# A two-layer decoder trunk on one NeuronCore: the per-layer gates in two halves of 512 columns, and p loaded earlier

## The reference, cut to what matters

```python
x = layer_norm(DEEPNORM_ALPHA * x + mix, ln1_g[i], ln1_b[i])
hid = jnp.square(jax.nn.relu(jnp.einsum('bsd,df->bsf', x, ffn_w1[i])))
x = layer_norm(DEEPNORM_ALPHA * x + jnp.einsum('bsf,fd->bsd', hid, ffn_w2[i]), ln2_g[i], ln2_b[i])
gate = jax.nn.sigmoid(jnp.einsum('bsd,de->bse', x, ple_gate_w[i]))
x = x + gate * jnp.einsum('bsk,kd->bsd', p[i], ple_w[i])
```

## Time and profile before

| | |
|---|---|
| median of 3 runs | 2124.36 us (2123.57 to 2124.47) |
| profiled execution | 2122.74 us, its span 2121.0 us |
| TensorE busy | 2102.9 us, 99% of the span |
| VectorE, ScalarE, GpSimd busy | 1270.7, 792.8, 733.5 us |
| granted TensorE clock | 1.00 (2.4 GHz) |
| chain of waits that ended last | PE 91%, DVE 3%, DMA 2% |

### The profile page before, as it was taken

How to read it: one execution, slowest core, us unless ns; L and a number is a source line. 1 busy time by engine, 2 the same in 40 slices (tenths; PEclk the granted TensorE clock), 3 DMA queues, 4 the chain that set the end, 5 groups by cost and what they waited for, 6 DMA issues and landing times.

```text
span 2121.0 us, 27192 instructions
## 1 busy us (share of the span) xinstructions
PE 2102.9 (99%) x10565; PEld 1786.2 (84%) x10565; DVE 1270.7 (60%) x1747; ACT 792.8 (37%) x1197; POOL 733.5 (35%) x493
## 2 busy tenths in 40 slices
PE   9999999999999999999999999999999999999999
PEld 9887788888888888899888888788888888888899
DVE  5744776565667666565543352676556667666564
ACT  3112464544544334521211101454454543344521
POOL 5112157777512000212432222258777512000220
PEclk9999999999999999999999999999999999999999
DMA  5121124444599743301121111124444599643311
GB/s 184 39 62 46 35 80 149 141 148 163 180 361 380 248 155 129 129 26 46 41 80 40 57 43 48 32 80 161 155 141 148 203 381 378 228 131 130 129 38 73
DMA packets 185948, 287.31 MB, mean 135 GB/s; under 512 B 12800, under 2 KB 82524, under 8 KB 185820
## 3 DMA queue, kind: packets, MB, share of 16 engines
q1 hardware_dynamic: 185120, 285.26, 39.4%
q10 hardware_dynamic: 700, 0.31, 0.1%
HBM read 221.56 MB, written 63.96 MB: 135 GB/s over the span
## 4 chain that ended last, share of the span: by engine, by line
PE 91%; DVE 3%; DMA 2%; issue 1%; POOL 1%; ACT 1%; SPq 0%; DVEq 0%; POOLq 0%; ACTq 0%
PE bank_a L1785 16%; PE bank_a L1787 16%; PE bank_a L1786 16%; PE bank_b L1785 14%; PE bank_b L1787 14%; PE bank_b L1786 14%; PE bank_a L1824 1%; DMA w_raw<-in_ffn_w_dram 1%; DMA p_n<-in_p_dram 1%; PE bank_b L1824 1%; DVE xt_lo L1339 0%; DVE xt_hi L1334 0%; POOL op_lo L983 0%; PE bank_a L1994 0%; DMA h_spill<-h_tile 0%
## 5 line engine op out<-in xcount | busy, mean ns | idle before, releaser
L968 POOL TENSOR_TENSOR w_lo<-raw,w_hi 128x512 fp32r<-128x512 f32 x160 | 226.3, 1446 | 986.0 <-ACT w_hi L1072 985.9
L1785 PE MATMUL bank_a<-xt_hi,w_hi 128*128 128x512 f32 x640 | 251.4, 393 | 2.7 <-DVE xt_lo L1339 2.7
L1787 PE MATMUL bank_a<-xt_hi,w_lo 128*128 128x512 f32 x640 | 249.2, 389 | 0.0
L1786 PE MATMUL bank_a<-xt_lo,w_hi 128*128 128x512 f32 x640 | 249.1, 389 | 0.0
L1526 DVE TENSOR_TENSOR hop_lo<-h_raw,hop_hi 128x1024 fp32r<-128x1024 f32 x112 | 141.6, 1265 | 141.8 <-ACT hop_hi L1165 141.6
L1165 ACT CAST hop_hi<-h_raw 128x1024 fp32r<-128x1024 f32 x112 | 117.7, 1051 | 237.4 <-PE bank_a L1787 140.6
L1785 PE MATMUL bank_a<-wop_hi,hop_hi 128*128 128x512 f32 x512 | 199.3, 389 | 0.7 <-DVE resid L1551 0.7
L1786 PE MATMUL bank_a<-wop_lo,hop_hi 128*128 128x512 f32 x512 | 199.2, 389 | 0.0
L1787 PE MATMUL bank_a<-wop_hi,hop_lo 128*128 128x512 f32 x512 | 199.2, 389 | 0.0
L1072 ACT CAST w_hi<-raw 128x512 fp32r<-128x512 f32 x160 | 88.2, 620 | 266.1 <-PE bank_a L1787 154.7
L1785 PE MATMUL bank_b<-w_hi,xt_hi 128*128 128x256 f32 x640 | 182.4, 285 | 2.3 <-DVE xt_lo L1339 1.7
(11 more groups left out here) (190 smaller groups left out, 4961.9 us busy)
## 6 DMA issues: line engine op xcount, KB each, us to landing
w_raw<-in_ffn_w_dram SPq DMA_DIRECT2D x144, 512.0 KB, 7.6
h_raw<-h_spill SPq DMA_DIRECT2D x112, 512.0 KB, 6.5
h_spill<-h_tile SPq DMA_DIRECT2D x170, 256.0 KB, 2.2
w_raw<-in_ffn_w_dram SPq DMA_DIRECT2D x112, 256.0 KB, 3.5
raw<-in_od_w_in_dram SPq DMA_DIRECT2D x48, 256.0 KB, 2.8
raw<-in_ple_gate_w_dram SPq DMA_DIRECT2D x32, 256.0 KB, 4.8
h_spill<-h_tile2t SPq DMA_DIRECT2D x28, 256.0 KB, 2.0
raw<-in_ev_w_in_dram SPq DMA_DIRECT2D x24, 256.0 KB, 3.1
```

Of the source, the lines that this page charges most:

```text
L968: pool.tensor_tensor(w_lo[slab % 2][:, s], raw[:, n % NRAW, :], w_hi[slab % 2][:, s].bitcast(F32), ALU.subtract).then_inc(lo_split, 1)
L1785: pe.matmul(dst, s_hi, m_hi, start=first, stop=False, skip_group_check=on_top)
L1786: pe.matmul(dst, s_hi, m_lo, start=False, stop=False, skip_group_check=on_top)
L1787: return pe.matmul(dst, s_lo, m_hi, start=False, stop=last, skip_group_check=on_top)
```

## The change

The gates of a layer are computed in two halves of 512 columns. A half's weights are ten pieces (eight of the gate's, two of p's), each 128 rows by 512 columns. A tile's gate product takes a whole bank and its p product the next one. The first half's pieces lie in the two slabs; six of the second half's lie in new places between 152 and 176 KB and four in the second slab, which TensorE gives back piece by piece during the last tile of the first half (`gate_step`). The sigmoid's buffer is twice as wide. p's load moves from `second` to the front of `slab`, and the turning of its first half from inside the last item to behind item 53. Because p then lies in 168 to 176 KB from there on, the w2 pieces of the last form take turns in 128 and 132 alone. ScalarE splits the second slab once item 55 is prepared, where it waited for item 55's difference alone. In layer 1 the stores go by halves. The diff, cut to its core:

```diff
@@ -189,7 +189,7 @@
     def w_chunk(self, load):
         if load < self.first_load[LAST_FORM]:
             return (184, 188, 32, 36, 168, 172, 176, 180)[load % 8]
-        return (128, 168, 172, 132, 128, 132, 168, 172)[load - self.first_load[LAST_FORM]]
+        return (128, 132)[(load - self.first_load[LAST_FORM]) % 2]
 
     def w_landed(self, load):
         return load % 8, 16 * (self.layer * self.loads // 8 + load // 8 + 1)
...
@@ -273,7 +273,7 @@
         st.need_x, st.need_h, st.turned = list(need["xu"]), list(need["hu"]), list(turned)
         adds = dict(ADDS.get(kind, {}))
         if kind in ("out", "gate", "v"):
-            adds["gb"] = adds["bread"] = len(args["tiles"]) * (2 if kind == "out" else 1)
+            adds["gb"] = adds["bread"] = len(args["tiles"]) * (1 if kind == "v" else 2)
             if kind == "gate":
                 adds["xnew"] = len(args["tiles"])
             if args.get("sums") is not None:
...
@@ -434,9 +434,9 @@
             if i == LAST_FORM + 3:
                 add("slab", layer=layer, load_next=True, split_next=True)
             if i == LAST_FORM + 5:
+                add("turn_p", half=0, layer=layer)
                 add("second", layer=layer)
-        st.inner = [add("turn_p", half=0, layer=layer, nested=True, early=True)]
-        squares_of(hi).inner = st.inner
+        squares_of(hi)
         add("stats", half=1, ln=ln)
         add("norm", half=1, ln=ln)
 
@@ -453,16 +453,25 @@
         add("prep", item=n, layer=layer)
 
     def gates(layer):
-        for c in range(4):
-            slab = ("gate", layer, c)
-            if c == 0:
-                token_halves("gate", slab, "ln", ln=2 * layer + 1, p=True, layer=layer, col=c)
-                continue
-            add("gate", slab=slab, tiles=lo, col=c, layer=layer)
-            if c == 3 and layer == 0:
-                last_half("gate", "gate", layer=layer, col=c)
-            else:
-                add("gate", tiles=hi, col=c, layer=layer, last=True)
+        add("more", slab=("gate", layer, 0), split_next=False, load_next=False)
+        add("gate", slab=("gate", layer, 1), tiles=[0, 1], layer=layer, split_next=False, load_next=False)
+        add("gload", layer=layer)
+        inner = [turns("ln", 1, list(range(KT)), ln=2 * layer + 1, nested=True)]
+        inner.append(add("turn_p", half=1, layer=layer, nested=True))
+        add("gate", tiles=[2, 3], inner=inner, layer=layer)
+        add("gsplit", item=0, layer=layer)
+        add("gate", tiles=hi[:-1], layer=layer)
+        add("gsplit", item=1, layer=layer)
+        add("gate", tiles=hi[-1:], layer=layer)
+        for _ in range(3):
+            slab_end.append(("gb", at["gb"]))
+        for c in (2, 3):
+            add("more", slab=("gate", layer, c), split_next=False, load_next=False)
+        st = add("gate", tiles=lo, col=1, layer=layer, split_next=True, load_next=True)
+        if layer == 0:
+            last_half("gate", "gate", layer=layer, col=1)
+        else:
+            add("gate", tiles=hi, col=1, layer=layer, last=True)
 
 
...
@@ -557,6 +566,9 @@
         tmp = at("tmp", [P, NTMP, HALF], 176 * K1)
         gb_rows = at("gb_rows", [P, 2, D], 192 * K1)
         shared = at("shared", [P, 512], 200 * K1)
+        sig = at("sig", [P, 2, HALF], 200 * K1)
+        g_hi = [at(f"g_hi{k}", [P, PIECE], a * K1, F32R) for k, a in enumerate((152, 156, 160, 164, 168, 172))]
+        g_lo = [at(f"g_lo{k}", [P, PIECE], a * K1, F32R) for k, a in enumerate((154, 158, 162, 166, 170, 174))]
         ws_t = at("ws_t", [P, 4, P], 202 * K1)
         ident = at("ident", [P, P], 206 * K1)
         small = 206 * K1 + 512
...
@@ -710,6 +722,21 @@
 
             q, f = {"A11": (0, 0), "A12": (1, 0), "A21": (0, 1), "A22": (1, 1)}[op]
             return w1_raw[b % 2][:, 4 * q:4 * q + 4, f * P:(f + 1) * P]
+
+        def piece_place(slab, q):
+
+            kind = slabs[slab][0]
+            if kind[0] == "gate" and kind[2] >= 2:
+                q += 5 * (kind[2] - 2)
+                if q < len(g_hi):
+                    return g_hi[q][:, :], g_lo[q][:, :]
+                slab, q = slab // 2 * 2 + 1, q - len(g_hi)
+            s = slice(q * PIECE, (q + 1) * PIECE)
+            return w_hi[slab % 2][:, s], w_lo[slab % 2][:, s]
+
+        def gate_slab(layer, c):
+
+            return next(i for i, (kind, _) in enumerate(slabs) if kind == ("gate", layer, c))
 
         def by_four(ap):
             return ap[:, :].rearrange("p (q f) -> p q f", q=4)
...
@@ -752,8 +779,9 @@
                     return row_slab(ev_w_out[0], what[1])
                 if kind == "od_out":
                     return row_slab(od_w_out[0], what[1])
-                ple = ple_w[what[1]].rearrange("(k p) n -> p k n", p=P)
-                return column_slab(ple_gate_w[what[1]], what[2] * BLK) + [ple[:, :, bass.ds(what[2] * BLK, BLK)]]
+                half, ks = what[2] // 2, range(5 * (what[2] % 2), 5 * (what[2] % 2) + 5)
+                return [(ple_gate_w if k < KT else ple_w)[what[1]][bass.ds(k % KT * P, P), half * HALF:(half + 1) * HALF]
+                        for k in ks]
 
             def load_slab(what, piece):
                 for q, src in enumerate(sources(what)):
...
@@ -843,13 +871,15 @@
                 if st.kind == "slab":
 
                     sp.wait_ge(ahead_dve, ahead[st.layer].dve[LAST_FORM - 1])
+                    sp.dma_start(p_n[:, :, :], p[st.layer, 0].rearrange("(t q) k -> q t k", q=P)).then_inc(p_in, 16)
                 if st.load_next and st.cur + 1 < n_slabs:
                     load_slab(*slabs[st.cur + 1])
+                if st.kind == "gload":
+                    load_slab(slabs[st.cur + 1][0], st.piece)
+                    load_slab(slabs[st.cur + 2][0], st.piece + 5)
                 if st.kind == "second":
-
                     load_slab(slabs[st.cur + 2][0], st.piece + 5)
                     sp.wait_ge(ahead_dve, ahead[st.layer].dve[-1])
-                    sp.dma_start(p_n[:, :, :], p[st.layer, 0].rearrange("(t q) k -> q t k", q=P)).then_inc(p_in, 16)
                     load_gb(ln2_g[st.layer], ln2_b[st.layer], D)
                 if st.kind == "ffn":
                     for k in range(2):
...
@@ -997,6 +1026,11 @@
                     split_low(st.cur + 2, st.piece + 4, 4)
                 if st.kind == "second":
                     split_low(st.cur + 2, st.piece + 5, 5)
+                if st.kind == "gsplit" and st.item == 0:
+                    split_low(st.cur + 1, st.piece, 5)
+                    split_low(st.cur + 2, st.piece + 5, 1)
+                if st.kind == "gsplit" and st.item == 1:
+                    split_low(st.cur + 2, st.piece + 6, 4, at=1)
                 if st.kind == "wsum" and ITEMS[st.item][0] == "m6":
                     a, i = ahead[st.layer], st.item
                     for n in range(2):
...
@@ -1136,8 +1170,19 @@
                 fifth = st.split_next and st.cur + 1 < n_slabs and slabs[st.cur + 1][0][0] == "gate"
                 if st.kind == "split":
                     split_high(st.cur + 2, st.piece + 4, 4, slab_end[st.cur])
+                if st.kind == "gsplit" and st.item == 0:
+                    split_high(st.cur + 1, st.piece, 5)
+                    split_high(st.cur + 2, st.piece + 5, 1)
+                if st.kind == "gsplit" and st.item == 1:
+                    for q in range(4):
+
+                        if q == 2:
+                            act.wait_ge(b_full, st.gb + 1)
+                        else:
+                            act.wait_ge(gate_step, 3 * st.layer + min(q, 2) + 1)
+                        split_high(st.cur + 2, st.piece + 6 + q, 1, at=1 + q)
                 if st.kind == "second":
-                    act.wait_ge(ahead_dve, ahead[st.layer].sum[-1])
+                    act.wait_ge(ahead_dve, ahead[st.layer].dve[-1])
                     split_high(st.cur + 2, st.piece + 5, 4)
                     split_high(st.cur + 2, st.piece + 9, 1, at=4)
                 if st.kind == "consts":
...
@@ -1291,14 +1336,14 @@
                         if k == len(st.tiles) - 1:
                             for turn in st.inner if len(st.tiles) == HT else ():
                                 values(turn)
-                        act.wait_ge(b_full, st.gb + k + 1)
+                        act.wait_ge(b_full, st.gb + 2 * k + 1)
                         if st.xnew + k >= 2:
 
                             act.wait_ge(x_new, st.xnew + k - 1)
                         else:
 
                             act.wait_ge(a_full, st.ga)
-                        act.activation(sig[:, (st.xnew + k) % 2, :], bank_b[(st.gb + k) % RING][:, 0:BLK],
+                        act.activation(sig[:, (st.xnew + k) % 2, :], bank_b[(st.gb + 2 * k) % RING][:, :],
                                        ACT.Sigmoid).then_inc(sig_ready, 1)
                 if fifth:
                     split_high(st.cur + 1, st.piece + 4, 1, at=4)
...
@@ -1760,10 +1802,10 @@
```

(61 more changed lines are left out.)

17 lines of the change are left out of this document (4 added, 13 removed).

## The result

The changed kernel takes 2128.8 us (median of 17 runs, 2127.39 to 2129.93) where the kernel before takes 2124.3 on the same chip (17 runs, 2121.19 to 2126.45): a ratio of 1.0022, 95% interval 1.0015 to 1.003. It is slower, by 4.5 us, and the forecast was 2133.1 in a range of 2122 to 2142. The profiled execution is 2129.59 us around a span of 2127.9; against before's profiled 2122.74 that is 6.9 us more.

The account below looks back on a forecast made before the run. TensorE, busy 2102.9 of 2121.0 us, was taken to bound the kernel. The terms -12.8 - 4.0 + 16.4 + 5.0 + 2.6 + 1.0 + 0.5 sum to +8.7 us, giving 2133.1 us, range 2122 to 2142.

Parts of the forecast that it names:

- the likeliest case: The forecast itself, without any rival: 2133.1 us, own range 2129 to 2138, chance 0.48.
- Wide matmuls: Both gates: 1920 matmuls of 256 columns become 960 of 512, each saving 13.3 ns, -12.8 us.
- Rival 4: Gates: the 13.3 ns go with columns, so a wide matmul costs two narrow ones; 2145.9 us, chance 0.02.
- p: Last product: TensorE's waits for p between second and third tile go as p comes earlier, -4.0 us.
- late next: Last product: once p is early, item 55's operand is what TensorE waits for; counted as +2.6 us.
- The flush: Item 48: two w2 places delay m7's flush on VectorE by four turns of 7.66 us; 8.2 per layer, +16.4 us.
- The restart: After the 8 us gap at item 48 TensorE resumes at half clock; 2.5 us per layer, +5.0 us.
- rival 1: Item 48: the clock holds through the 8 us gap; +3.7, 2128.1 us, chance 0.25.
- Item 55: Last product: queued gate loads and ScalarE's fifth-piece cast delay item 55's operand; 1.3 per layer, +2.6 us.
- Tile 4: Gates: tile 4 waits for tile 2's banks, which VectorE reads late; 0.5 per layer, +1.0 us.
- the end: Kernel's end: the multiply and add are 0.27 us longer each and the store twice as large; +0.5 us.
- Rival 2: Item 48: the flush stall does not come; -15.3, 2109.1 us, chance 0.12.

Follow-up runs that it names:

- e1: The changed kernel with p loaded and turned where it was and four w2 places again, only the wide gates new: 2110.06 us, ratio 0.9945.
- e5: The changed kernel with four w2 places again for items 48 to 55 and p's load behind item 50's preparation: 2111.1 us, ratio 0.9947.
- e4: The changed kernel with VectorE's flush of m7 ahead of item 52's difference and item 51's preparation, two places kept: 2110.83 us, ratio 0.9939.
- e2: The kernel before with w2 of the last form in two places and the ScalarE wait this needs: 2152.15 us, ratio 1.0135.
- e3: The changed kernel with 27 unread matmuls of 512 columns issued by TensorE just before item 48: 2124.06 us, ratio 1.0003.
- e6: e4's kernel with ScalarE's cast of the gate slab's fifth raw piece moved behind item 55's preparation: 2108.25 us, ratio 0.9933.
- e7: The changed kernel with only the cast of the fifth raw piece moved behind item 55's preparation: 2125.07 us, ratio 1.001.
- e8: The changed kernel with four w2 places, m7's flush first and the fifth cast behind item 55: 2108.03 us, ratio 0.9932.

## Why the prediction was right

The forecast said slower by the chain from two places to a late flush, and the runs confirm each link. The size was less well met: the medians differ by 4.5 us where I forecast 8.7, and 2128.8 lies just under the 2129 to 2138 that I gave the likeliest case. By its steps:

- **Wide matmuls, -12.8 us.** The gates are shorter by 11.4 with the tile-4 waits of 0.76 inside, so -12.2. The pitch of the earlier trace rows holds in the gates (24 steps in 5.44 us). Rival 4 is out.
- **p, -4.0 us.** Right as a wait that goes. What the forecast listed as "late next" took 3.2 of it back in the same place; e1 and e5 show the edit's worth as none.
- **The flush, +16.4 us forecast, 13.4 measured.** The mechanism and the four turns were right, the turn was 7.1 to 7.4 us and not 7.66. The mis-sized term is the landing: the four in question leave VectorE idle 2.74 to 3.94 us, and five loads of that stretch land in 3.7 (median), where I took 4.1 from four rows of 3.8 to 4.6. Four turns with 0.4 too much each are 1.6 us per layer, the whole difference; my 0.15 for the two semaphores, given without a row, comes out at about 0.12 (7.12, 7.43 and 7.23 less the landings of 3.6, 3.9 and 3.7 and VectorE's 3.41). The 3.8, which was one of my ends (7.1 per layer), was nearest; the 4.6 came with more traffic. e4 and e5 take it away in two independent ways, e2 makes it alone.
- **The restart, +5.0 forecast, 4.7 measured.** Judged from the opening's pitch, against a granted clock that read 1.00 there, and that was right: the 1.00 was no reading (last section), so the column spoke for rival 1 only over a kernel without a long wait. In mid-kernel the column shows the fall (0.50), and e3 that idleness causes it. Rival 1, which had 0.25, is out; its time of 2128.1 lies nearer to the median measured than my forecast because the flush was 3 us cheaper and the executions differ.
- **Item 55, +2.6 forecast, 3.2 measured.** e6 and e7 show that the fifth piece's cast is what holds it. In layer 0 TensorE is there at 885.5 (884.8 forecast) and the operand at 887.1 (886.1). The fifth cast ends at 883.11, near the 882.7, but from ScalarE's first cast of item 55 to the end of VectorE's wop_lo it is 4.1 us and not 3.4: hop_lo takes 1.88 us in place of 1.22, and what slows it isn't shown. My sum left the restart out of both times. It cancels: in e3, which has none, the fifth cast comes 2.4 us sooner and TensorE 2.1, and the wait is 1.4 in place of 1.7.
- **Tile 4, +1.0 forecast, 0.8 measured; the end, +0.5, measured 0.6.**

Rival 2 (2109.1, no flush stall) is what e4 and e5 built, and they came to 2110.8 and 2111.1: had the order of VectorE been another, the same change would have been 0.6% faster. The sum of my terms was 1.8 us over the profiled pair's 6.9. The rest of the 4.3 us between forecast and median is the executions: the profiled pair differs by 6.9, the medians by 4.5.

## What to carry to other kernels

When an edit takes buffers from a ring of loads, write out one turn of the ring (load, everything the consumer does in its order until the buffer is free, load again) and compare it with the pace of the bound engine; then ask which instruction that has nothing to do with those loads stands behind the waiting one. Two of four places made a turn of 7.2 us against a pace of 5.44, and the price was not in the items loaded but in a flush queued behind them; moving that flush (e4) was worth as much as giving the places back (e5). Here each wait of TensorE of 3.7 us or more cost its length and then matmuls at half clock, so of a few long waits and many short ones the long ones go first; a short one isn't always free of it (e3's opening below).

## What the runs showed of the hardware

- TensorE came back at the lower clock after each idle time of 6 to 7 us (six of six: item 48 in both layers of the changed kernel, of e2 and of e7), with 6 to 13 matmuls at 427 ns before the pitch of 227 returned, 1.3 to 2.7 us lost; and after both of p's in e2 (3.7 and 4.3 us). After the 2.53 us of the earlier trace rows it kept 227 ns. The last wait's length doesn't decide it alone: in the opening of e3 the clock fell just behind a wait of 1.90 us, while TensorE was working again. The rows, and the window with the granted clock third from the end:

```profile
14.62 0.28 PE L1829 MATMUL bank_b<-w_hi,xt_lo 128*128 128x256 f32 x1
16.80 0.39 PE L1827 MATMUL bank_b<-w_hi,xt_hi 128*128 128x256 f32 x1 [1.90 <-DVE xt_lo L1384]
...
18.56 0.41 PE L1828 MATMUL bank_b<-w_lo,xt_hi 128*128 128x256 f32 x1
20.48 0.36 PE L1828 MATMUL bank_b<-w_lo,xt_hi 128*128 128x256 f32 x1
...
17.20:20.60 3.40, 3.35 (x16) 3.06 (x16) 2.46 (x5) 0.00 (x0) 0.04 (x1) 0.50 1.07 366
```

- The mean granted clock goes with the time of an execution. Beside e1 to e8 the kernel before ran 32 times: 19 times at 1.000, 2120.4 to 2123.8 us (median 2122.1), and 13 times at 0.999 or less, 2122.5 to 2126.8 (median 2124.0). All twenty executions of e4, e5, e6 and e8, in which TensorE waits neither for p nor at item 48, had 1.000. This would fit a clock that falls at before's wait for p in some executions; it isn't shown, since before's trace is of an execution at 1.000, and e3's trace shows a fall in the opening.
- At the lower clock the pitch of a 512-wide matmul is 426 ns, 512 columns at 1.2 GHz (426.7) and nothing on top, and that of a 256-wide one 213 (nine steps in 1.92 us from 18.56 in e3 above, 213.3 by its columns). At the upper they are 226.7 and 120.0, each 13.3 more than its columns. The 13.3 ns that the wide gates save exist at 2.4 GHz alone. The Trainium skill (TensorE: Matmul & The Clock Gate, Part 1) states the same asymmetry, a fixed cost that shows only when warm, but puts it at about 2.5 ns; the traces agree with the form and not with the size.
- In the opening the granted clock reads 1.00 over transposes at half pace because nothing was recorded there: the first clock entry in the trace of the kernel before begins 7.3 us into the span, and the view counts time without an entry as full. The pitch agrees with the entry: 16 transposes take 3.47 us from start to start at first and 1.74 from 7.92 on, and the 2.87 of the 16 between them put the change at 7.3. In e5 the entry comes at 5.4, and there the second 16 take 2.08. Where an entry exists, clock and pitch agree in each of the places above; in the first microseconds only the pitch tells.
